# Projecting keys and values of a neighbourhood attention as one 512-column panel, with token rows as the stationary operand

## The chip, the cores and the metric

The kernel runs on one core of a Trainium2 chip. The metric is the device time of one execution in microseconds (us); the time before the change is the median of 3 runs. The compute engines are TensorE (PE in the rows; its weight loads PEld), VectorE (DVE), ScalarE (ACT) and GpSimd (POOL); SP only issues transfers.

## What is computed

Two transformer blocks in float32 over 256 tokens of width 2048. The first block (three mixers, an MLP of width 8192) and the second block's gated convolutional feed-forward are not touched. The change is in the second block's neighbourhood attention, over 256 tokens and 256 context rows, with 16 heads of 128:

```
def project(t):
    q, k, v = jnp.split(t @ w_qkv, 3, axis=-1)
    sh = (t.shape[0], t.shape[1], NA_HEADS, HEAD_DIM_2)
    return rms_norm(q.reshape(sh), q_g), rms_norm(k.reshape(sh), k_g), v.reshape(sh)

q, k, v = project(h)          # h: 256 own rows
qc, kc, vc = project(hc)      # hc: 256 context rows; only kc, vc are used
...
    logits = q @ [own keys, context keys] * scale + bias (own keys only)
    out = softmax(logits) @ [own values, context values]
y = out @ w_o
```

`c` and `c_ctx` go through `silu(cond) @ w_ada + b` (2048 x 12288) to give shifts, scales and gates; this product is worked on by VectorE beside the rest, piece by piece.

## The kernel before

**Weights as units.** All weights come as units of 128 x 1024 floats (512 KB) through a ring of four slots. For each unit SP loads `raw`, ScalarE copies it to `whi` (line 723, a rounded float32r), VectorE writes the rest `raw - whi` to `wlo` (line 1227), and TensorE uses it three times: whi with the high part of the activations, whi with their low part, wlo with the high part. `split(u0, m + 3)` on ScalarE may begin once TensorE is through with the unit three before (`unit_used`), on VectorE once `hi_done` says so; SP may refill `raw` after `lo_done`. The engines take their instructions in program order, and each program is written by hand: what stands behind a waiting instruction waits too.

**The attention phase** takes 8 turns of two heads each (`na_turn`), 12 units a turn: 4 of keys, 4 of queries, 4 of values, each 256 columns wide and 4 chunks of the contraction deep. Keys (units 0 to 3, lines 2486 and 2493) and queries (4 to 7, line 2498) have the weights stationary and the tokens moving, so that they come out turned, a head's 128 numbers on the partitions; keys move 512 tokens at a time, except in the last chunk and in the first turn (`first_keys`, line 2396), where own and context tokens stand apart and move 256. Values (8 to 11, line 2505) have 128 tokens stationary and 256 weight columns moving. Because a key's 128 numbers lie across partitions, the sums of squares for its norm come from a product with ones: ScalarE squares twice (1073, 1074), VectorE forms the low part (1779), TensorE multiplies (`norm_sums`, 2456 and 2457), ScalarE takes Ln and Exp (1057, 1059), VectorE scales (1744, 1748).

The attention of a turn's heads runs in the next turn: `attend_p(i, m)` behind unit m has the score product (2425), the transposes of the probabilities (2434) and the product with the values (2447); `attend_v` and `attend_a` are its halves on VectorE and ScalarE. The last turn's attention runs between the first units of `w_o` (`WO_UNITS`, line 1993, 32 units in four column groups n = 0 to 3, of 8 units each; a group adds into PSUM area q = n % 2).

**The w_ada product.** In each turn VectorE adds 32 terms (line 1559, 128x384) from 8 blocks of 4 terms. POOL loads a block (768 KB, line 655) into one of two buffers when the block two before is used up; behind the eighth load of a turn it adds a mask to the bias (661). `ada_tail` says which terms stand in which unit's slot. Behind the attention phase 16 more terms lie in `ffn_gate(j)`.

**The way into w_o.** The products with `w_o` need the heads' outputs in a high and a low part: ScalarE makes the high one (`heads_hi`, 1095), POOL the low one (689), in chunks; the units of group 0 wait for them (`a_lo`). VectorE adds a finished group to the residual (`add_gated`, 1827 and 1829), and the group two further on may not begin before 1827 has read the area (`drained`).

Of the kernel before, what the change touches and what calls it, by code (L numbers as in the profile page):

```python
# [19 lines left out]
F32 = mybir.dt.float32  # L20
F32R = mybir.dt.float32r
ACT = mybir.ActivationFunctionType
ALU = mybir.AluOpType
# [95 lines left out]
NA_OWN = 36  # L119
# [46 lines left out]
def program(nc, t, out):  # L166
    ctx = ExitStack()
    with ctx:
# [38 lines left out]
        ones_r = sb("ones_r", [P, P], F32R)  # L207


        with nc.sbuf_tensor("cst", [P, NCONST], F32) as cst, nc.sbuf_tensor("arena", [P, 17152], F32) as arena:  # L210
            pass
        first_dead = CONST["tri"][0]
        sb("kept_consts", [P, first_dead])
        nsq_hi = sb("nsq_hi", [P, 1024], F32R)
        sb("other_areas", [P, NCONST - first_dead - 1024 + 9472])
        nsq_lo = sb("nsq_lo", [P, 1024], F32R)
        sb("last_areas", [P, 17152 - 9472 - 1024])
# [56 lines left out]
        kT = area(4096, 2, 2 * S)  # L274
        vv = area(5120, 4, S)
# [4 lines left out]
        nsq = area(9472, 1024)  # L280
        nrs = area(10496, 1024)
# [46 lines left out]
        lr_ok = [sem(f"lr_ok{i}") for i in range(RING)]  # L328
# [39 lines left out]
        n_sq, n_nsum, n_rs, n_norm = (sem("na_" + n) for n in ("sq", "nsum", "rs", "norm"))  # L368
        n_sqa = sem("na_squares")
# [12 lines left out]
        D_NA = (D_MLP[0], D_MLP[1] + 8)  # L382
# [42 lines left out]
        def _(sp):  # L425
# [17 lines left out]
            for n, (name, c0, w) in enumerate(PANELS_IN):  # L443
                for j in range(8):
                    u = 8 * n + j
                    if name == "BV0":
# [4 lines left out]
                        sp.dma_start(dst[:, :, 0:LR], w_in[:, 2 * j:2 * j + 2, 3584:3600]).then_inc(lr_ok[j % RING], 16)  # L451
# [42 lines left out]
            with sp.Fori(1, 9) as i:  # L494
                for j in range(12):
                    first = (D, 0, 2 * D)[j // 4]
                    load(i * 12 + (U_NA - 12), j, raw[:, j % RING, :].rearrange("p (k n) -> p k n", n=256),
                         wq[:, 4 * (j % 4):4 * (j % 4) + 4, bass.ds(i * 256 + (first - 256), 256)])
            wo = t["na_w_o_2"][0].rearrange("(k p) n -> p k n", p=P)
            for i, (n, j) in enumerate(WO_UNITS):  # L500
                wide(U_WO, i, 512, wo[:, 2 * j:2 * j + 2, 512 * n:512 * n + 512])
# [197 lines left out]
        def _(act):  # L699
# [10 lines left out]
            act.sem_inc(n_rs, AHEAD)  # L710
# [165 lines left out]
            for m in range(8 * len(PANELS_IN)):  # L876
# [3 lines left out]
                if n < len(PANELS_IN):  # L880
                    name, _, w = PANELS_IN[n]
                    split(8 * n, j, w, (lr_ok[j % RING], 16 * (j // RING + 1)) if name == "BV0" else None)
                else:
                    split(8 * n, j)
# [94 lines left out]

            def turn_step(e, at):  # L980
# [14 lines left out]
            for j in range(4, 35):  # L995
                split(U_MLP + 3 * 64 + 32, j)
# [23 lines left out]
            split(U_NA, 3)  # L1020
# [10 lines left out]

            act.activation(ones_r[:, :], ones, ACT.Copy)
# [20 lines left out]
            def inv_rms(i, r):  # L1053
                v = nrs[:, 512 * (r % 2):512 * (r % 2) + 512]
                act.wait_ge(n_nsum, i * 3 + (r + 1))
                act.wait_ge(n_norm, i * 3 + ((1 if r == 2 else 0) + AHEAD))
                act.activation(v, X[2], ACT.Ln, scale=1.0 / NHD, bias=EPS).then_inc(n_rs, 1)
                act.wait_ge(n_rs, i * 6 + (2 * r + 1 + AHEAD))
                act.activation(v, v, ACT.Exp, scale=-0.5).then_inc(n_rs, 1)

            def na_turn(i, first):
                u0 = i * 12 + U_NA
                for m in range(12):
                    if not (first and m == 0):
                        split(u0, m + 3)
                    if m == 0 and not first:
                        act.wait_ge(unit_used, u0)
                        act.activation(vv, Gf[1].rearrange("p (c t) -> p c t", t=S), ACT.Copy).then_inc(drained[1], 1)
                    if not first:
                        attend_a(i, m)  # L1070
# [4 lines left out]
                    if m == 6:  # L1075
                        if first:
                            act.wait_ge(x2_ok, 1)
                        inv_rms(i, 0)
                    if m == 7:
                        inv_rms(i, 1)  # L1080
                    if m == 8:
                        act.wait_ge(unit_used, u0 + 8)
                        act.activation(nsq[:, 0:512], X[0], ACT.Square)
                        act.activation(nsq_hi[:, 0:512], X[0], ACT.Square).then_inc(n_sqa, 1)
                    if m == 10:
                        inv_rms(i, 2)

            na_turn(0, True)
            with act.Fori(1, 8) as i:
                na_turn(i, False)  # L1090
# [8 lines left out]
            act.wait_ge(unit_used, U_WO)  # L1099
            act.activation(vv, Gf[1].rearrange("p (c t) -> p c t", t=S), ACT.Copy).then_inc(drained[1], 1)  # L1100
            split(U_WO, 3)
            for m in range(7):
                attend_a(8, m, 1)
                if m < 6:
                    split(U_WO, 4 + m)
# [1523 lines left out]
```

## Time and profile before

| | |
|---|---|
| median of 3 runs | 2479.31 us (2478.68 to 2480.09) |
| the profiled execution's own time | 2479.1 us |
| its span | 2477.3 us |
| PE busy, granted clock | 2466.0 us (100%), 1.0 (2.4 GHz) in every stage read |
| DVE busy | 1781.5 us (72%) |
| ACT busy | 1183.1 us (48%) |
| POOL busy | 219.4 us (9%) |
| DMA | 519.08 MB, mean 210 GB/s |

The span lies 1.8 us inside the run's time. Busy time of PE is an envelope of overlapping matmuls, so a busy PE says little by itself; the order of its work and the waits in it have to be read.

### The profile page before, as it was taken

Reading aid. Unit: us, or ns where it says so; the run is one execution under the profiler, and the core shown is the slowest. Engines: PE = TensorE matmul, PEld = TensorE weight load, DVE = VectorE, ACT = ScalarE, POOL = GpSimd, SP = SyncE. Lnnn points to the kernel's source line nnn. Section 1 sums busy time; section 2 is a strip of 40 time slices with the busy share of each in tenths; the row PEclk is TensorE's granted clock in tenths of the full one; section 3 lists DMA queues with packets and bytes.
Section 4 is the critical chain, followed back from the end, with each engine's and each line's share of the span. In section 5 each row is a group of like instructions: output and inputs, shape, how many; then the busy total and the mean of one; then the engine's idle time right before and its main releaser. Section 6 shows DMA issues by size and latency. Waiting matters only on the chain.

```text
span 2477.3 us, 39343 instructions
## 1 busy us (share of the span) xinstructions
PE 2466.0 (100%) x14118; PEld 2156.9 (87%) x14118; DVE 1781.5 (72%) x2227; ACT 1183.1 (48%) x1517; POOL 219.4 (9%) x251
## 2 busy tenths in 40 slices
PE   9999999999999999999999999999999999999999
PEld 8989988888888888889999999988888888888887
DVE  6667657798887887786777777776766656665666
ACT  4455555544534535555333333354655435553453
POOL 5000000000000000223111111130200000000000
PEclk9999999999999999999999999999999999999999
DMA  8655577887787787764765565666556665566655
GB/s 270 186 132 150 172 247 231 296 278 254 240 285 243 249 282 238 259 213 151 219 189 188 186 194 183 199 211 191 189 179 197 193 191 181 182 198 193 187 182 173
DMA packets 279545, 519.08 MB, mean 210 GB/s; under 512 B 32750, under 2 KB 102648, under 8 KB 278672
## 3 DMA queue, kind: packets, MB, share of 16 engines
q1 hardware_dynamic: 254128, 403.66, 51.7%
q0 software_dynamic: 25120, 113.89, 14.8%
q8 instruction: 75, 1.23, 0.2%
q14 instruction: 30, 0.25, 0.0%
q10 hardware_dynamic: 192, 0.05, 0.0%
HBM read 515.35 MB, written 6.90 MB: 211 GB/s over the span
## 4 chain that ended last, share of the span: by engine, by line
PE 95%; DVE 2%; DMA 1%; issue 1%; ACT 0%; POOL 0%; DVEq 0%; ACTq 0%; POOLq 0%
PE ps L1993 33%; PE ps L2022 22%; PE ps L2025 11%; PE ps L2505 7%; PE ps L2493 6%; PE ps L2498 4%; PE ps L1985 3%; PE ps L2447 1%; PE ps L2425 1%; PE ps L2396 1%; DVE wlo L1227 1%; PE ps L2314 1%; PE ps L2434 1%; PE ps L2486 0%; DMA raw<-in_w_in 0%
## 5 line engine op out<-in xcount | busy, mean ns | idle before, releaser
L1227 DVE TENSOR_TENSOR wlo<-raw,whi 128x1024 fp32r<-128x1024 f32 (+1 forms) x776 | 939.6, 1222 | 419.0 <-ACT whi L723 402.3
L723 ACT ACTIVATE whi<-raw 128x1024 fp32r<-128x1024 f32 (+1 forms) x776 | 798.5, 1037 | 797.3 <-PE ps L1993 355.2
L1993 PE MATMUL ps<-whi,act 128*128 128x512 f32 (+3 forms) x2736 | 821.9, 382 | 0.9 <-DVE wlo L1227 0.9
L2022 PE MATMUL ps<-act,whi 128*128 128x512 f32 x2400 | 657.6, 395 | 1.4 <-DVE act L1867 1.3
L1993 PEld LDWEIGHTS ps<-whi,act 128*128 128x128 f32 x2736 | 504.4, 188 | 92.2 <-issue 3.2
L1993 PE MATMUL ps<-wlo,act 128*128 128x512 f32 (+3 forms) x1368 | 519.3, 380 | 0.0
L2022 PEld LDWEIGHTS ps<-act,whi 128*128 128x128 f32 x2400 | 410.1, 189 | 56.6 <-DVE act L1867 1.6
L2025 PEld LDWEIGHTS ps<-act,wlo 128*128 128x128 f32 x2400 | 369.5, 189 | 51.7
L2025 PE MATMUL ps<-act,wlo 128*128 128x256 f32 x2400 | 383.9, 281 | 0.0
L1993 PEld LDWEIGHTS ps<-wlo,act 128*128 128x128 f32 x1368 | 256.9, 188 | 45.1
L1559 DVE SCALAR_TENSOR_TENSOR arena<-arena,cond 128x768 f32<-128x768 f32 (+1 forms) x330 | 284.2, 884 | 12.2 <-DMA arena<-in_w_ada 8.9
L2505 PE MATMUL ps<-whi,act 128*128 128x256 f32 x1024 | 185.8, 284 | 0.0
L2505 PEld LDWEIGHTS ps<-whi,act 128*128 128x128 f32 x1024 | 160.3, 191 | 1.4
L2505 PE MATMUL ps<-wlo,act 128*128 128x256 f32 x512 | 144.9, 283 | 0.0
L2493 PE MATMUL ps<-act,whi 128*128 128x512 f32 x420 | 131.7, 395 | 0.0
L601 POOL DMA_DIRECT2D arena<-in_w_ada x64 | 46.4, 724 | 663.8 <-DVEq L1577 586.8
L2505 PEld LDWEIGHTS ps<-wlo,act 128*128 128x128 f32 x512 | 97.8, 191 | 0.0
L1038 ACT ACTIVATE arena<-arena,nst 128x512 f32<-128x512 f32 x32 | 23.2, 726 | 155.3 <-DVE nst L1732 155.3
L1985 PE MATMUL ps<-act,whi 128*128 128x256 f32 x512 | 95.5, 287 | 0.6 <-DVE act L1246 0.6
L2498 PE MATMUL ps<-act,whi 128*128 128x256 f32 x512 | 95.0, 286 | 0.0
L1906 DVE SCALAR_TENSOR_TENSOR arena<-arena,cols 128x255 f32<-128x255 f32 x172 | 71.9, 480 | 31.6 <-ACT arena L1162 28.0
L2493 PEld LDWEIGHTS ps<-act,whi 128*128 128x128 f32 x420 | 76.9, 188 | 14.8
(332 smaller groups left out, 2142.1 us busy)
## 6 DMA issues: line engine op xcount, KB each, us to landing
arena<-in_w_ada POOLq DMA_DIRECT2D x128, 768.0 KB, 6.1
raw<-in_ffn_w_up SPq DMA_DIRECT2D x160, 512.0 KB, 4.2
raw<-in_w_mlp_in SPq DMA_DIRECT2D x128, 512.0 KB, 4.9
raw<-in_w_mlp_out SPq DMA_DIRECT2D x128, 512.0 KB, 5.5
raw<-in_na_w_qkv SPq DMA_DIRECT2D x96, 512.0 KB, 4.7
raw<-in_ffn_w_down SPq DMA_DIRECT2D x84, 512.0 KB, 4.4
raw<-in_w_in SPq DMA_DIRECT2D x64, 384.0 KB, 3.8
raw<-in_w_in SPq DMA_DIRECT2D x32, 512.0 KB, 4.4
```

Source lines behind the costliest of these rows:

```text
L601: pool.dma_start(ada1[:, e % 4, :, :], wa[:, 2 * e:2 * e + 2, bass.ds(s * ADA_W, ADA_W)])\
L723: act.activation(a, b, ACT.Copy).then_inc(hi_done, 1)
L1227: dve.tensor_tensor(a, b, c, ALU.subtract).then_inc(lo_done, 1)
L1559: return dve.scalar_tensor_tensor(out=acc, in0=piece, scalar=sc, in1=acc, op0=ALU.mult, op1=ALU.add)
L1906: ins = dve.scalar_tensor_tensor(out=a, in0=b, scalar=w, in1=a, op0=ALU.mult, op1=ALU.add)
L1985: ins = pe.matmul(o, a, b, start=start and i == 0, stop=last and i == 2, skip_group_check=True)
L1993: ins = pe.matmul(o, a, b, start=start and i == 0, stop=last and i == 2, skip_group_check=True)
L2022: pe.matmul(Z[q][:, c, :].rearrange("p (h t) -> p h t", h=2), kn(whi, j)[:, kk, P * c:P * c + P], act2[:, :, k, 0:S], start=k == 0, stop=k ...
L2025: ins = pe.matmul(Z[q][:, c, 0:S], kn(wlo, j)[:, kk, P * c:P * c + P], ahi[:, k, 0:S], start=False, stop=k == KC - 1, skip_group_check=True)
L2493: ins = pe.matmul(G[0][:, c, :], a, b, start=st and y == 0, stop=False, skip_group_check=True)
L2498: ins = pe.matmul(X[0][:, S * c:S * c + S], a, b, start=st and y == 0 and c == 0, stop=sp_ and y == 2, skip_group_check=True)
L2505: ins = pe.matmul(Gf[1][:, S * r:S * r + S], a, b, start=st and y == 0 and r % 2 == 0, stop=sp_ and y == 2, skip_group_check=True)
```

## The change

Keys and values become one panel: a unit holds 2 chunks of the contraction and 512 columns (256 of keys, 256 of values), and with 128 tokens stationary the 512 columns move past. Units 0 to 7 are such panels, over four token tiles, in PSUM banks 0 to 3; units 8 to 11 are the queries, also with tokens stationary. Each panel unit is loaded by two transfers, with a semaphore (`part_ok`) beside `raw_full`; so are the first three units of `w_o`. Keys and queries now lie with a token's numbers along a row: VectorE sums the squares there (`row_sums`), ScalarE makes the factor, VectorE scales, and TensorE turns the result head by head (`turn_keys` behind unit 10, `turn_queries` behind unit 0 of the next turn), 8 and 4 transposes; the gains are applied by the copies out of PSUM (`k_out`, `q_out`). The product with ones is gone. The attention of a turn begins one unit later; the last turn's begins behind unit 2 of `w_o`, not ahead of unit 0. The w_ada terms are placed anew (`FIRST_TERMS`, `TURN_TERMS`, `ffn_gate`), and groups 0 and 1 of `w_o` end only at units 14 and 15.

```
-WO_UNITS = [(n, j) for n in range(4) for j in range(8)]
-WO_UNITS[7], WO_UNITS[8] = WO_UNITS[8], WO_UNITS[7]
-FIRST_TERMS = {7: range(16, 19), 8: range(19, 23), 9: range(23, 27), 10: range(27, 30), 11: range(30, 32)}
+WO_UNITS = [(n, j) for n in (0, 1) for j in range(7)] + [(0, 7), (1, 7)] + [(n, j) for n in (2, 3) for j in range(8)]
+FIRST_TERMS = {3: range(16, 19), 4: range(19, 22), 5: range(22, 25), 6: range(25, 28), 7: range(28, 32)}
+TURN_TERMS = [range(0, 3), range(3, 6), range(6, 9), range(9, 12), range(12, 15), range(15, 19), range(19, 23), range(23, 28),
+              range(28, 29), range(29, 30), range(30, 31), range(31, 32)]
...
# ScalarE, the turn
-                    if m == 4:
-                        act.wait_ge(unit_used, u0 + 4)
-                        act.activation(nsq, Gf[0], ACT.Square)
-                        act.activation(nsq_hi[:, :], Gf[0], ACT.Square).then_inc(n_sqa, 1)
...
                     if m == 8:
                         act.wait_ge(unit_used, u0 + 8)
+                        if not first:
+                            act.wait_ge(n_o, i * 4 + AHEAD)
+                        for r in range(4):
+                            act.activation(kv[:, r, :], ps[:, r, :], ACT.Copy).then_inc(k_row, 1)
+                    if m == 9:
+                        inv_rms(16, k_rms, i * 2 + 1, 8)
+                    if m == 11:
+                        act.wait_ge(k_turn, i + 1)
+                        act.activation(kT, ps[:, 5:7, :], ACT.Copy, scale=cols[:, R_KG:R_KG + 1]).then_inc(k_out, 1)
...
# VectorE, the turn
+            def row_sums(rows_, sums, r):
+                for a in range(2):
+                    at = 2 * r + a
+                    v = rows_[:, NHD * a:NHD * a + NHD]
+                    if at >= 4:
+                        own.wait(3)
+                    own.mark(dve.tensor_tensor_reduce(n_junk[:, at % 4, :], v, v, 1.0, 0.0, ALU.mult, ALU.add,
+                                                      nst[:, sums + at:sums + at + 1]))
...
+                    if m == 8:
+                        key_sums(i)
+                    if m == 9:
+                        key_norm(i)
...
-                        attend_v(i, m)
-                        ada_tail(i, m)
+                        if m == 0:
+                            query_norm(i)
+                        else:
+                            attend_v(i, m - 1)
+                        ada_terms(i, TURN_TERMS[m])
...
# VectorE beside w_o
-                if 11 <= j < 19:
-                    ada_terms(8, range(2 * j - 22, 2 * j - 20))
+                if 13 <= j < 19:
+                    ada_terms(8, ((0, 1, 2), (3, 4, 5), (6, 7, 8), (9, 10, 11), (12, 13), (14, 15))[j - 13])
...
-                if j % 8 == 3:
-                    n = j // 8 - 1
+                if j in (18, 19, 27):
+                    n = (18, 19, 27).index(j)
                     dve.wait_ge(gate_in, 16)
-                    add_gated(n, n % 2, U_WO + (9 if n == 0 else 8 * n + 8), drained[n % 2], D_NA[n % 2] + n // 2 + 1, gb)
+                    add_gated(n, n % 2, U_WO + (15, 16, 24)[n], drained[n % 2], D_NA[n % 2] + n // 2 + 1, gb)
...
# TensorE
+            def key_value_unit(m, tiles):
+                for kk in range(2):
+                    k = 2 * m + kk
+                    wh, wl = kn(whi, m)[:, kk, :], kn(wlo, m)[:, kk, :]
+                    for r in tiles:
+                        for y, (a, b) in enumerate(terms(wh, wl, tile_rows(r, 0, k), tile_rows(r, 1, k), False)):
+                            ins = pe.matmul(ps[:, r, :], a, b, start=k == 0 and y == 0, stop=k == KC - 1 and y == 2,
+                                            skip_group_check=True)
+                return ins
...
             def first_keys():
-                pe.wait_ge(drained[0], D_MLP[0])
+                for q in range(2):
+                    pe.wait_ge(drained[q], D_MLP[q])
...
-                if i < 6:
-                    attend_p(8, i + 1, 1)
+                if i == 1:
+                    turn_queries(8)
+                if 2 <= i <= 8:
+                    attend_p(8, i - 2, 1)
```

VectorE in the first turn, from slot 7 (a split, L1227 before and L1240 now; the w_ada terms are L1559 before and L1572 now). Before:

```order
L1227 TENSOR_TENSOR wlo<-raw,whi 128x1024 [waits hi_done]
L1744 SCALAR_TENSOR_TENSOR arena<-ps,cols,arena 128x512 [waits na_rs]
L1227 TENSOR_TENSOR wlo<-raw,whi 128x1024 [waits hi_done]
L1558 TENSOR_SCALAR arena<-arena,cond 128x384 [waits ada_in0]
L1559 SCALAR_TENSOR_TENSOR arena<-arena,cond 128x384 [waits dve_step] x2
L1744 SCALAR_TENSOR_TENSOR arena<-ps,cols,arena 128x512 [waits na_rs,dve_step]
```

Now, with the sums of squares as L1759 (the row of the sum and the row of its accumulator) and the scaling as L1766:

```order
L1240 TENSOR_TENSOR wlo<-raw,whi 128x1024 [waits hi_done,ada_done]
L1572 SCALAR_TENSOR_TENSOR arena<-arena,cond 128x384 [waits ada_in1]
L1572 SCALAR_TENSOR_TENSOR arena<-arena,cond 128x384 [waits dve_step] x3
L1240 TENSOR_TENSOR wlo<-raw,whi 128x1024 [waits hi_done,ada_done]
L1759 ISA arena,nst<-arena 128x128 [waits na_keys_rows]
L1759 ISA nst 128x1
```

```order
L1240 TENSOR_TENSOR wlo<-raw,whi 128x1024 [waits dve_step,hi_done]
L1766 TENSOR_TENSOR arena<-arena,nst 128x4x256 [waits na_keys_sums_rms]
L1240 TENSOR_TENSOR wlo<-raw,whi 128x1024 [waits hi_done] x2
L159 UNCONDITIONAL_BRANCH
L159 ISA
```

The keys' norm used to stand ahead of most terms; now all 16 terms of this turn, with the wait for the last block (`ada_in1`), stand ahead of the eight sums and of the scaling.

TensorE in the turn, behind the third of the last four units (queries now, values before). Before:

```order
L2505 MATMUL ps<-wlo,act2 128x256
L2456 MATMUL ps<-nsq_hi,ones_r 128x512 [waits na_rs,na_pt,na_sq]
L2457 MATMUL ps<-nsq_lo,ones_r 128x512
L2505 MATMUL ps<-whi,act2 128x256 [waits lo_done]
L2505 MATMUL ps<-whi,act2 128x256
```

Now:

```order
L2483 MATMUL ps<-cst,arena 128x128 [waits na_pt,na_logits,na_keys_scaled]
L2483 MATMUL ps<-cst,arena 128x128 x7
L2527 REGISTER_ALU
L2446 MATMUL ps<-whi,act2 128x256 [waits lo_done]
L2446 MATMUL ps<-whi,act2 128x256
```

At this place TensorE now waits for the scaled keys of the same turn.

VectorE beside w_o, around the first add of a finished group (L1827 before, L1863 now). Before:

```order
L1807 TENSOR_TENSOR act2<-arena,act2 128x2x256 [waits a_hi,a_lo]
L1227 TENSOR_TENSOR wlo<-raw,whi 128x1024 [waits hi_done] x2
L1827 TENSOR_TENSOR arena<-ps,arena 128x1024 [waits unit_used,gate_rows_in]
L1829 TENSOR_TENSOR x<-x,arena 128x2x512 [waits drained0]
L1558 TENSOR_SCALAR acc3<-arena,cond 128x384 [waits dve_step,ada_in0]
```

Now:

```order
L1240 TENSOR_TENSOR wlo<-raw,whi 128x1024 [waits hi_done,dve_step]
L1572 SCALAR_TENSOR_TENSOR acc3<-arena,cond,acc3 128x384
L1572 SCALAR_TENSOR_TENSOR acc3<-arena,cond,acc3 128x384 [waits dve_step] x2
L1240 TENSOR_TENSOR wlo<-raw,whi 128x1024 [waits hi_done,ada_done]
L1572 SCALAR_TENSOR_TENSOR acc3<-arena,cond,acc3 128x384 [waits ada_in1]
L1572 SCALAR_TENSOR_TENSOR acc3<-arena,cond,acc3 128x384 [waits dve_step]
L1240 TENSOR_TENSOR wlo<-raw,whi 128x1024 [waits hi_done,dve_step]
L1863 TENSOR_TENSOR arena<-ps,arena 128x1024 [waits unit_used,gate_rows_in]
L1865 TENSOR_TENSOR x<-x,arena 128x2x512 [waits drained0]
```

The add of group 0 stood ahead of all 16 terms; it now stands behind 14 of them.

## Rows read from the trace of the kernel before

**Rows 1.** The page: shares of the chain that ended last

```profile
PE 95%; DVE 2%; DMA 1%; issue 1%; ACT 0%; POOL 0%; DVEq 0%; ACTq 0%; POOLq 0%
```

**Rows 2.** Waits in the attention phase and w_o, longest first (total, times, longest)

```profile
PE ps L2425 <- DVE arena L1729: 1.4, 3, 0.5
...
PE ps L1993 <- DVE wlo L1227: 0.3, 1, 0.3
```

**Rows 3.** The chain in order of time, in a turn (start, us, work)

```profile
1343.82 2.87 PE ps L2498 x24
...
1384.73 5.49 PE ps L2493 x24
1390.22 0.86 PE ps L2425 x2
1391.08 0.44 PE ps L2434 x4
```

**Rows 4.** The chain where the MLP hands over to the first turn

```profile
1113.50 1.42 DVE x L1544 x2
...
1118.03 0.21 ACT frms L1016
...
1119.24 1.06 PE ps L2386 x8
```

**Rows 5.** VectorE in order of time, one turn (start, us, operation, idle before)

```profile
1228.24 2.58 DVE L1559 SCALAR_TENSOR_TENSOR arena<-arena,cond 128x384 f32<-128x384 f32 x4
1232.26 2.92 DVE L1227 TENSOR_TENSOR wlo<-raw,whi 128x1024 fp32r<-128x1024 f32 x1 [1.44 <-ACT whi L723]
```

**Rows 6.** POOL in the same turn

```profile
1231.46 0.75 POOL L655 DMA_DIRECT2D arena<-in_w_ada  x1 [4.64 <-DVE arena L1559]
1232.23 1.85 POOL L661 TENSOR_TENSOR arena<-arena,cst 128x768 f32<-128x768 f32 x1
```

**Rows 7.** Row sums of squares, 128x192 (min/median/max ns, first and last start)

```profile
L1434 DVE CUSTOM_DVE_ANT_0 arena<-x x8: 352/354/355, 287.9 to 289.8; 128x192 f32<-128x192 f32 x8
```

**Rows 8.** Loads of w_ada blocks: from turn 2 on; then those beside w_o

```profile
DMA to landing us min/median/max: 4.9/5.2/7.6
DMA to landing us min/median/max: 7.6/7.6/7.6
```

**Rows 9.** First turn: loads of blocks 5, 6 and 7, and POOL's last issues

```profile
DMA to landing us min/median/max: 9.5/9.5/9.5
DMA to landing us min/median/max: 8.5/8.5/8.5
DMA to landing us min/median/max: 10.9/10.9/10.9
1166.61 0.75 POOL L655 DMA_DIRECT2D arena<-in_w_ada  x1 [4.97 <-issue]
1169.16 1.19 POOL L671 DMA_DIRECT2D gate_row_scratch<-mods  x1
```

**Rows 10.** w_o with the last attention: VectorE, ScalarE, POOL

```profile
1650.68 0.42 DVE L1727 SCALAR_TENSOR_TENSOR arena<-ps,arena 128x256 f32<-128x256 f32 x1
1654.04 0.71 ACT L1095 ACTIVATE act<-arena 128x256 fp32r<-128x256 f32 x2
1654.53 2.14 POOL L689 TENSOR_TENSOR act<-arena,act 128x256 fp32r<-128x256 f32 x2 [3.38 <-ACT act L1095]
```

**Rows 11.** VectorE in the later part of w_o

```profile
1689.69 1.22 DVE L1227 TENSOR_TENSOR wlo<-raw,whi 128x1024 fp32r<-128x1024 f32 x1
1690.84 1.26 DVE L1559 SCALAR_TENSOR_TENSOR acc<-arena,cond,acc 128x384 f32<-128x384 f32 x2
...
1697.63 1.27 DVE L1559 SCALAR_TENSOR_TENSOR acc<-arena,cond,acc 128x384 f32<-128x384 f32 x2 [1.83 <-DMA arena<-in_w_ada]
...
1707.41 1.22 DVE L1827 TENSOR_TENSOR arena<-ps,arena 128x1024 f32<-128x1024 f32 x1
```

**Rows 12.** The chain in w_o: three units in a row, behind the attention

```profile
1675.18 8.22 PE ps L1993 x36
```

More of the change, by code:

```diff
@@ L366, in program @@
             ("bias", "scores", "logits", "max", "exp", "probs", "turned", "pt", "pv", "out"))
[L368 to L369 removed]
+        k_row, k_rms, k_norm, k_turn, k_out = (sem("na_keys_" + n) for n in ("rows", "sums_rms", "scaled", "turned", "out"))
+        q_row, q_rms, q_norm, q_turn, q_out = (sem("na_query_" + n) for n in ("rows", "sums_rms", "scaled", "turned", "out"))
         gate_cols, gate_out, gate_in = sem("gate_columns"), sem("gate_row_out"), sem("gate_rows_in")
@@ L1019, in _ @@
             scale_piece(1, xs, xs, frms[:, 1, 0:1])
-            split(U_NA, 3)
+            split(U_NA, 3, extra=key_part(0, 3))
             turn_step(4, 0)
@@ L1671, in _ @@
                     own.done(ins)
-            own.done(dve.tensor_tensor_reduce(ps[:, 3, :], xs[:, 1, cs3], xs[:, 1, cs3], 1.0, 0.0, ALU.mult, ALU.add, fsq[:, 3, 3:4]))
+            own.done(dve.tensor_tensor_reduce(area(7424, 512), xs[:, 1, cs3], xs[:, 1, cs3], 1.0, 0.0, ALU.mult, ALU.add, fsq[:, 3, 3:4]))
             dve.wait_ge(fsq_ok, 1)
@@ new lines, in rows_scaled, with query_norm @@
+            def rows_scaled(v, sums, n, done):
+                by = nst[:, sums + n:sums + 2 * n].rearrange("p (r h) -> p r h", h=2).unsqueeze(3).to_broadcast([P, n // 2, 2, NHD])
+                v = v.rearrange("p r (h n) -> p r h n", n=NHD)
+                dve.tensor_tensor(v, v, by, ALU.mult).then_inc(done, 1)
+            def query_norm(i):
+                dve.wait_ge(q_row, i)
+                for r in range(RT):
+                    row_sums(qr[:, r, :], 32, r)
+                own.wait()
+                dve.sem_inc(q_rms, 1)
+                dve.wait_ge(q_rms, i * 2)
+                rows_scaled(qr, 32, 4, q_norm)
@@ L1755, in ada_terms, with key_sums, key_norm @@
+            def key_sums(i):
+                for r in range(4):
+                    dve.wait_ge(k_row, i * 4 + (r + 1))
+                    row_sums(kv[:, r, 0:S], 16, r)
+                own.wait()
+                dve.sem_inc(k_rms, 1)
+            def key_norm(i):
+                dve.wait_ge(k_rms, i * 2 + 2)
+                rows_scaled(kv[:, :, 0:S], 16, 8, k_norm)
             def ada_terms(i, ks):
@@ L2507, in na_turn @@
-                    ins.then_inc(unit_used, 1)
-                    if not first:
-                        attend_p(i, m)
-                    if m == 0:
+                    pe.wait_ge(lo_done, u0 + (m + 1))
+                    if first and m < 8:
+                        pe.wait_ge(a_lo, TURN_AT[4] + 2 * m + 2)
+                    if m < 8:
+                        key_value_unit(m, range(4)).then_inc(unit_used, 1)
+                    else:
+                        if m == 8 and not first:
+                            pe.wait_ge(q_row, i)
+                        query_unit(m)
@@ L2516, in na_turn @@
                     if m == 10:
-                        norm_sums(i, 2)
+                        turn_keys(i, first)
             na_turn(0, True)
```

273 lines of the change are left out of this document (112 added, 161 removed).

## The prediction, written before the changed kernel was run

> **What bounds the kernel now.** First the page's shares of the chain that ended last: TensorE holds 95% of it [rows 1]. Then the waits of the attention phase: from the first turn to the end of w_o TensorE waits four times, 1.4 us for VectorE's logits and 0.3 for weights, all in w_o [rows 2]. Then the chain in order of time, which gives the pitch at which TensorE takes each kind of work at full clock: 24 matmuls of 512 columns in 5.49 us are 0.228 us each, 24 of 256 columns in 2.87 us are 0.120 us, a product with ones, as wide, the same, a score product 0.86 us, four transposes 0.44 us, 0.11 each [rows 3]. In w_o 36 matmuls of 512 columns take 8.22 us, again 0.228 [rows 12]. So in the turns TensorE's own list of work is the time, and each microsecond taken from it counts, as long as nothing new makes it wait. VectorE is busy 49 of a turn's 67 us, but in bursts, and its order decides below.
>
> **The work on TensorE.** A steady turn before has 90 projection matmuls of 512 columns and 300 of 256: 20.5 + 36.0 = 56.5 us. Now 192 of 512 and 96 of 256: 43.8 + 11.5 = 55.3 us. The columns streamed are the same; what is saved is 0.012 us for each of 102 pairs of 256 that became one of 512, 1.2 us. Six products with ones (1.4 us) go, twelve transposes (1.3 us) come. Net -1.25 us a turn, -8.8 us over seven. In the first turn all 480 matmuls were 256 wide (57.6 us), so 2.3 us are saved, 1.4 go and 8 transposes (0.9) come: -2.8 us. The last queries' four transposes fall into w_o: +0.4 us. Sum -11.2 us, and this would be the result if every wait were covered. The Trainium skill speaks against the saving: its page "TensorE: Matmul & The Clock Gate", section "Back-to-back issue gap", puts an isolated gap at the columns over 2.4 plus about 2.5 ns, by which a pair would save 2.5 ns and a turn 0.3 us. The rows show 12 ns a pair, so the rows stand [rows 3].
>
> **The hand-over into the first turn, +1.5 us.** Before, TensorE went from the last MLP matmul straight into the first context half, since only area 0 had to be free. Now it waits for `drained[1]` as well, which VectorE sets behind its last add, 1.42 us from 1113.50 [rows 4]. The other wait there, for the scaled rows, ended at 1119.24 just as two context halves had run; it no longer adds anything, as TensorE arrives later.
>
> **Turning the keys in a steady turn, +2.2 us each.** Unit 7 starts at 0, when the last product with the values is done. TensorE: unit 7 to 5.5, unit 8 and one w_ada turn to 8.7, units 9 and 10 to 14.4; then `turn_keys` wants the scaled keys. VectorE was waiting in slot 6 for that same product, since the copy of the output stands ahead of slot 6's terms. From 0: copy 0.45, terms 19 to 22 at 0.645 each [rows 5], 19 done at 1.1 and all at 3.05, split 1.14 (back to back), term 23 at 4.85. Term 24 needs block 6, whose load POOL can issue once term 19 is done. POOL takes 0.64 us to react (terms that end at 1230.82, issue at 1231.46 [rows 5, 6]), and a block lands 5.2 us later [rows 8]: 6.9. Meanwhile POOL issues block 7 (term 23 frees it, 5.5 to 6.25) and adds the mask, 1.85 us, to 8.1. That mask add has a price: the split that met it took 2.92 instead of 1.22 us, till 1.1 us behind POOL's end [rows 5, 6]. The four terms will now meet it, so they begin at 8.1 and end at 10.7. Then split 11, to 11.85; eight row sums, for which 128x192 gives a pitch of (289.8-287.9)/7 = 0.27 us [rows 7], less 64 elements, 0.21: 13.55; ScalarE's Ln and Exp, 0.45 [rows 4], beside term 28 to 14.2; split 12 to 15.4; the scaling of 128x1024, priced as a split of that size, to 16.6. TensorE waits 2.2 us, more than the 1.25 saved: +0.95 a turn, +6.7 over seven.
> Bounds: if the mask does not hold the terms up, the wait is 1.0 us and the turn gains 0.3; if block 6 were there in time as well, no wait and -1.25; with the 7.6 us landing [rows 8] the wait is 3.5. I take the block, as both operations read two SBUF operands like the split. The skill's page "SBUF — State Buffer", section "SBUF: two separate sides", says so: a VectorE operation with two SBUF inputs and a GpSimd one that reads SBUF lock each other out for a whole instruction. The split's row agrees with it; that a term is held the same way no single row shows.
> The two transfers in place of one for each panel unit cost nothing that I can see: they move the same bytes in the same 1 KB pieces, and are issued in the slot four ahead of ScalarE's use, behind which a 5 us landing hides; the extra wait on ScalarE falls on a semaphore long set. The queries' path holds: 5.5 us of unit 0 against split 1.1 + 1.2, sums 0.85, Ln/Exp 0.45, scaling 0.7, about 4.6 us.
>
> **Turning the keys in the first turn, +6.3 us.** All 16 terms stand ahead of the sums here. `x2_ok` frees POOL at about 1143, as before; block 5, issued at about 1144.8, lands 9.5 us later as it did [rows 9], so term 20 goes at 1154.3; three more terms and a split at the prices above put term 23's end at 1158.1 and block 7's issue at 1158.7. Before, this block needed 10.9 us, with the gate's row being written 2.55 us behind its issue [rows 9]; the same order stands on POOL now. Landed at 1169.6, terms 28 to 31 end at 1172.2, split 1173.3, sums 1175.0, split 1176.1, scaling 1177.3. TensorE, 1.5 us late at the start and then without a wait, wants them at 1171.0. Bounds: 0.5 us if the block lands in 5 us, 3.9 with block 6's 8.5 [rows 9].
>
> **w_o with the last attention, +2.3 us.** Unit j of group 0 needs chunks 2j and 2j+1 of the heads. Before, from VectorE's start on a score product to POOL's two low parts passed 5.99 us (1650.68 to 1656.67 [rows 10]), and TensorE had two units and two score products to fill it. Now the attention comes two units later but the chunks' places on ScalarE do not, so only one unit, a score product and transposes (about 3.9 us) stand between: unit 4 waits 2.4 us, units 2, 5 and 6 together 1 us. Unit 0 waits 1.0 us too, since `heads_hi` now stands behind the copy of the keys. Against these 4.4 us, the waits there before were 2.2 us (1.4 listed [rows 2], the rest in modelled ends). +2.2, rounded with the queries' turn 2.7 in all.
>
> **w_o, group 2, +5.6 us.** Call T the start of unit 9. TensorE reaches unit 16, the first of group 2, at T+19.2 (seven units of 2.74 [rows 12]) and needs the first half of `add_gated(0)`. VectorE: split 13 cannot end before T+5.1 (its high part needs unit 9's end); three terms 6.85; split 8.0; term 3 at 8.65, which frees block 2's buffer; issue 0.3 later as at 1689.97, landing 7.6 us [rows 8]: 16.6. Terms 4 to 7 and a split are done by 12.4; it waits. Term 8 at 17.25, split 18.4, three terms 20.35, split 21.5, two terms 22.8, split 23.95, then the multiply of 1.22 [rows 11]: 25.2. TensorE waits 6.0. Before, that add stood at unit 11, five units ahead of need, and its own wait for the block, 1.83 us idle [rows 11], was absorbed. With a landing of 5.2 the wait is 3.6. About 0.4 is given back where TensorE waited 0.3 us for weights [rows 2]: that wait is behind unit 16.
>
> **Sum.** -2.8 + 1.5 + 6.3 = +5.0 for the first turn, +6.7 for seven, +2.7 and +5.6 for w_o: +20.0 us on the profiled execution's 2479.1, 1.8 of which lie outside its span. It stands 0.2 below the median: 2499.
>
> **The rivals.** A change under 0.2% (5 us) cannot be told from none here.
> (1) Slower as above, the waits outweighing the work: 70%. Its own range 2485 to 2508.
> (2) Covered waits, faster: only the work and the hand-over count, -11.2 + 1.5, 2469. It would need the terms not to hold the norm, by block landings of under 4.2 us or a mask that costs nothing, and group 0's add in time. Against it: no landing of under 4.9 us in [rows 8], and group 2 waits 1.7 us even without any block wait. With some of the waits it ends between: 2469 to 2474. 15%.
> (3) The lower ends together: first turn -2.8 + 1.5 + 0.5, seven turns -2, w_o +2.7 + 3.2: +3, 2482. Within 0.2%. 15%.
> (4) The change doesn't save what it says, because 512 columns over the stationary rows take twice 0.120: +9.8 us on top, 2509. The same form runs at 0.228 in w_o [rows 12]; this is inside the slower chance, under 3%.
>
> **How the numbers follow.** Likeliest case 2499. The range reaches down to take in most of (3), 2478, and up to the longer landings (7 x 1.3 + 8 in w_o), 2508. Faster 0.15, same 0.15, slower 0.70.
>
> **What will show it.** In the changed profile: projection pieces of 5.48 us and 2.87 us, work per turn 66.1; TensorE idle behind unit 10 with the scaling (VectorE, the new line 1766) as releaser, about 2 us in seven turns and 4 to 6 in the first; a wait of 3 to 6 us at unit 16 of w_o for VectorE's 1863; a wait for the low parts before unit 4; a period of 68.3 us a turn against 67.3. I am wrong if the turn's period is 66.1 (the terms never hold the norm), or if the group wait is missing, which would mean blocks that land far sooner.

## The result, and the profile after

The changed kernel takes 2518.61 us (median of 4 runs, 2516.8 to 2520.29), the kernel before 2479.12 in the same comparison: a ratio of 1.0156, 95% interval 1.0144 to 1.0168. It is slower by 39.5 us where 20 were predicted, and lies outside the range given. In one of the runs below, run 10, one of 8 executions took 8167 us and is left out of the ratio.

TensorE's share of the chain that ended last, 95% before [rows 1], is now:

```profile
PE 88%; DVE 5%; DMA 4%; issue 2%; ACT 1%; POOL 0%; DVEq 0%; SPq 0%; POOLq 0%; ACTq 0%
```

TensorE's waits from the hand-over to the end of w_o (total, times, longest), where before there were 1.4 and 0.3 us [rows 2]:

```profile
PE ps L2483 <- DVE arena L1766: 21.1, 8, 3.4
PE ps L2029 <- POOL act L694: 5.7, 5, 2.5
PE ps L2472 <- DVE arena L1766: 5.0, 1, 5.0
PE ps L2029 <- DVE arena L1863: 5.0, 1, 5.0
PE ps L2435 <- issue: 1.6, 1, 1.6
```

Four of these five were predicted, with 21.7, 4.4, 6.0 and 1.5 us. The third was not: the turning of the first queries, behind unit 0 of turn 1. The stages, from the starts of the units in the chain, in microseconds of the profiled executions (the last one ends where TensorE begins the feed-forward's products, at 1749.3 before and at 1788.5 after):

| stage | before | after | more | predicted |
|---|---|---|---|---|
| to the start of turn 1 | 1176.1 | 1181.4 | +5.3 | +5.0 |
| turn 1 | 67.3 | 78.2 | +10.9 | +0.95 |
| turns 2 to 6 | 336.6 | 345.8 | +9.2 | +4.75 |
| turn 7 and w_o | 169.3 | 183.1 | +13.8 | +9.25 |

One steady turn in the chain in order of time, to set beside [rows 3]:

```profile
1378.44 4.89 DMA arena<-in_w_ada
1383.36 1.74 DVE arena L1572
...
1391.20 0.93 issue
1392.13 1.23 DVE arena L1766
1393.40 1.09 PE ps L2483 x8
1394.50 2.88 PE ps L2446 x24
1397.38 5.47 PE ps L2435 x24
```

This is the predicted path, link by link: block 6 lands, term 24 (1.74 us instead of 0.63) goes under the mask add, three terms, split, sums and scaling follow, and TensorE waits 2.52 us for it (2.2 predicted). Counted from the start of unit 7 at 1376.45, block 6 lands at 6.9, its four terms end at 10.6 and the scaling at 16.9, where the prediction has 6.9, 10.7 and 16.6. Around the first turn's end, ScalarE, and then POOL, in order of time:

```profile
1178.09 1.06 ACT L727 ACTIVATE whi<-raw 128x1024 fp32r<-128x1024 f32 x1 [5.11 <-DMA raw<-in_na_w_qkv]
1185.38 1.06 ACT L727 ACTIVATE whi<-raw 128x1024 fp32r<-128x1024 f32 x1 [6.23 <-DMA raw<-in_na_w_qkv]
...
1188.29 0.58 ACT L1069 ACTIVATE arena<-ps 128x512 f32<-128x512 f32 x1
```

```profile
1162.74 1.19 POOL L676 DMA_DIRECT2D gate_row_scratch<-mods  x1
```

ScalarE stands 11.3 us before weights that have not landed, and the copy of the queries' rows (1069) stands behind the second of these splits. The landing of the write at 1162.74 (8 KB, the gate's row), and of the second transfers of the units requested at 1164.6 and 1167.7:

```profile
DMA to landing us min/median/max: 12.5/12.5/12.5
```

```profile
DMA to landing us min/median/max: 13.4/15.5/17.6
```

Then TensorE's clock. The windows of the changed kernel (us, then busy time of PE, PEld, DVE, ACT, POOL; the last three numbers are granted clock, DMA share, GB/s), and two pieces of the chain:

```profile
1165.00:1170.00 5.00, 5.00 (x44) 5.00 (x43) 4.79 (x8) 1.98 (x4) 0.77 (x1) 1.00 0.42 29
1170.00:1175.00 5.00, 1.56 (x15) 1.36 (x13) 4.80 (x19) 0.42 (x2) 0.75 (x1) 0.86 0.50 32
1175.00:1180.00 5.00, 5.00 (x24) 5.00 (x25) 0.82 (x1) 1.06 (x1) 0.00 (x0) 0.50 0.96 283
...
1190.00:1195.00 5.00, 3.12 (x11) 2.84 (x12) 3.94 (x12) 2.15 (x4) 0.00 (x0) 0.57 0.47 157
```

```profile
1532.28 4.31 PE ps L2446 x24
```

```profile
1739.77 10.27 PE ps L2029 x36
```

Two things are to be seen. While the 8 KB write is under way the DMA engines are half busy (0.42 and 0.50) and move 29 to 32 GB/s. And behind TensorE's stall the granted clock is 0.50, its lower level (1.2 GHz), for a few microseconds: 24 matmuls of 256 columns take 4.31 us instead of 2.87 [rows 3], 36 of 512 take 10.27 instead of 8.22 [rows 12]. Such pieces stand behind the first turn's wait, the queries' wait in turn 1, the keys' wait of turns 1 and 5, and the wait of group 2.

### The profile page after: what moved, and what is told of

It is laid out like the page before. It is cut to its first block, busy times and chain, and to the rows that moved or that the text cites. A ratio compares the mean times of both kernels' runs of the same rounds, so it can differ in the third digit from the quotient of the medians.

```text
span 2516.6 us, 38054 instructions
## 1 busy us (share of the span) xinstructions
PE 2468.2 (98%) x13260; PEld 2119.8 (84%) x13260; DVE 1786.5 (71%) x2395; ACT 1161.1 (46%) x1512; POOL 218.1 (9%) x251
## 4 chain that ended last, share of the span: by engine, by line
PE 88%; DVE 5%; DMA 4%; issue 2%; ACT 1%; POOL 0%; DVEq 0%; SPq 0%; POOLq 0%; ACTq 0%
PE ps L2029 33%; PE ps L2058 22%; PE ps L2061 11%; PE ps L2435 11%; PE ps L2021 3%; DMA arena<-in_w_ada 2%; DVE arena L1572 2%; PE ps L2513 1%; PE ps L2494 1%; DVE wlo L1240 1%; PE ps L2446 1%; DMA raw<-in_na_w_qkv 1%; DMA raw<-in_w_in 1%; PE ps L2503 1%; PE ps L2350 0%
## 5 line engine op out<-in xcount | busy, mean ns | idle before, releaser
L1240 DVE TENSOR_TENSOR wlo<-raw,whi 128x1024 fp32r<-128x1024 f32 (+1 forms) x776 | 930.4, 1210 | 411.8 <-ACT whi L727 390.2
L2029 PE MATMUL ps<-whi,act 128*128 128x512 f32 (+3 forms) x2736 | 823.8, 382 | 11.3 <-POOL act L694 5.7
L2058 PE MATMUL ps<-act,whi 128*128 128x512 f32 x2400 | 657.6, 395 | 1.4 <-DVE act L1903 1.3
L2029 PEld LDWEIGHTS ps<-whi,act 128*128 128x128 f32 x2736 | 505.0, 188 | 104.5 <-POOL act L694 5.7
L2058 PEld LDWEIGHTS ps<-act,whi 128*128 128x128 f32 x2400 | 410.1, 189 | 56.6 <-DVE act L1903 1.6
L2435 PE MATMUL ps<-whi,act 128*128 128x512 f32 x1024 | 325.0, 399 | 1.6 <-issue 1.6
L1572 DVE SCALAR_TENSOR_TENSOR arena<-arena,cond 128x768 f32<-128x768 f32 (+1 forms) x330 | 291.2, 905 | 19.4 <-DMA arena<-in_w_ada 16.0
L2435 PEld LDWEIGHTS ps<-whi,act 128*128 128x128 f32 x1024 | 189.5, 189 | 42.1 <-issue 5.3
L2435 PE MATMUL ps<-wlo,act 128*128 128x512 f32 x512 | 201.1, 393 | 0.0
L606 POOL DMA_DIRECT2D arena<-in_w_ada x64 | 46.3, 724 | 665.0 <-DVEq L1590 588.2
L2446 PE MATMUL ps<-whi,act 128*128 128x256 f32 x512 | 98.8, 294 | 0.0
L2021 PE MATMUL ps<-act,whi 128*128 128x256 f32 x512 | 95.5, 287 | 0.6 <-DVE act L1259 0.6
L2446 PEld LDWEIGHTS ps<-whi,act 128*128 128x128 f32 x512 | 83.8, 199 | 0.6
L660 POOL DMA_DIRECT2D arena<-in_w_ada x64 | 48.2, 753 | 413.3 <-DVE acc L1572 226.3
```

Of the source, the lines that this page charges most:

```text
L606: pool.dma_start(ada1[:, e % 4, :, :], wa[:, 2 * e:2 * e + 2, bass.ds(s * ADA_W, ADA_W)])\
L660: pool.dma_start(ada2[:, q % 2, :, :], wa[:, 4 * c:4 * c + 4, bass.ds(i * 768 + (6144 + (s - 1) * TAIL_W), TAIL_W)])\
L1240: dve.tensor_tensor(a, b, c, ALU.subtract).then_inc(lo_done, 1)
L1572: return dve.scalar_tensor_tensor(out=acc, in0=piece, scalar=sc, in1=acc, op0=ALU.mult, op1=ALU.add)
L2021: ins = pe.matmul(o, a, b, start=start and i == 0, stop=last and i == 2, skip_group_check=True)
L2029: ins = pe.matmul(o, a, b, start=start and i == 0, stop=last and i == 2, skip_group_check=True)
```

## The experiments

Each is timed against the kernel before in the same comparison; its ratio is to that kernel. Where a time is said to be so many us less, it is less than the changed kernel's 2518.61 us. Letters A, B and C are the rivals of the expectation quoted.

**1. The gate row's write, later.**

```
             attention_loads(0, range(4, 8))
+            attention_loads(1)
             gate_row_out(0, 32)
-            with pool.Fori(1, 8) as i:
+            with pool.Fori(2, 8) as i:
```

> The changed kernel (2518.6 us) with one edit: the write of the gate's row (8 KB out of 128 partitions) is issued behind the loads of turn 1 instead of behind those of the first turn. Theory A: this write, which took about 12 us to land and began 6.4 us earlier than before the change, holds up the unit loads behind it; ScalarE's two waits for weights (11.3 us) and the 5.0 us of TensorE at the turning of the first queries come from it. Then turn 1 falls from 78.4 to 68.9 to 70 us, and the time by 8 to 10, to 2509 to 2511. Rival B: the loads are late because the w_ada blocks of the first turn are loaded earlier and the panel units come as two transfers; then turn 1 stays above 76 us and the time within 2 us of 2518.6. Rival C: the write does the same harm wherever it stands; then the loss moves to turn 2 and the time stays.

Measured: 2514.5 us, ratio 1.0148 (1.0131 to 1.0165), 4 us less. Turn 1 takes 74.0 us. The first transfers of the three units requested from 1164.5 to 1171.4 now land in:

```profile
DMA to landing us min/median/max: 3.0/5.0/5.9
```

and the queries' wait of 5.0 us is gone. But in turn 1 the keys' wait is 5.1 instead of 2.5. POOL, then VectorE, there:

```profile
1234.17 0.75 POOL L660 DMA_DIRECT2D arena<-in_w_ada  x1 [3.09 <-DVE arena L1573]
...
1236.73 1.19 POOL L676 DMA_DIRECT2D gate_row_scratch<-mods  x1
```

```profile
1245.30 0.62 DVE L1573 SCALAR_TENSOR_TENSOR arena<-arena,cond 128x384 f32<-128x384 f32 x1 [3.06 <-DMA arena<-in_w_ada]
```

Block 7, on its way when the write begins, takes 11 us, and the norm stands behind its first term. So A holds for what the write does at the first turn's end. The time lies between A's (8 to 10 us less) and C's (none), and the 4 us are hardly clear of noise: the four executions span 2512.87 to 2521.42 us. The write still harms what is in transit beside it and soon needed.

**2. Four terms behind the norm** (`TURN_TERMS` from slot 7: term 23; none; 24 to 27; 28 and 29; 30 and 31).

> The changed kernel with terms 24 to 27 of turns 1 to 7 moved behind the scaling of the keys (slot 9), 28 and 29 to slot 10, 30 and 31 to slot 11. Theory A: the 2.5 us wait of TensorE at the turning of the keys is the norm standing behind block 6 and its four terms; it vanishes in turns 1 to 7, a steady turn takes 66.2 us instead of 68.9, and with two places at which the granted clock had fallen behind that wait (1.5 us each) the time falls by 19 to 22 us, to 2497 to 2500. Rival B: the split for unit 11, now beside POOL's mask, takes the place of the terms and the scaling is late all the same: periods of 68, the time 2512 to 2516. Rival C: the late terms delay the next turn's first block, and the next turn's terms or splits hold TensorE up: periods of 67 to 69 with waits at another place.

Measured: 2514.79 us, ratio 1.0144 (1.0127 to 1.0161), against an expected 2497 to 2500: a miss. TensorE's waits in steady turns:

```profile
PE ps L2472 <- DVE arena L1766: 10.2, 5, 2.1
```

There is no wait for the keys any more, as A said, but one of 2.05 us for the queries, and a turn takes 68.4 us. Between the two scalings (of the keys, then of the queries) VectorE now has eight terms besides its splits, where it had three, and the queries' sums stand behind them. This is rival C, with a time in B's range. The norm has two deadlines in 10 us, and terms pushed past the first meet the second.

**3. The mask add behind block 5** (`if q == 5:` in place of 7).

> The changed kernel with POOL's mask add issued behind block 5 of a turn instead of block 7. Theory A (the step of the prediction): VectorE's terms 24 to 27 took 3.9 us instead of 2.6 because this add holds them; without it they take 2.6, TensorE's wait at the turning of the keys falls from 2.5 to about 1.2 us, a turn from 68.9 to 67.6, and the time by 9 to 12 us, to 2507 to 2510. Rival B: the terms are slow for another reason (they read a block that has just landed while others land): they stay at 3.9 us and the time within 2 us of 2518.6.

Measured: 2504.75 us, ratio 1.0102 (1.0085 to 1.0119), 13.9 less. VectorE's terms 24 to 27, in the changed kernel and in this one:

```profile
1383.36 3.69 DVE L1572 SCALAR_TENSOR_TENSOR arena<-arena,cond 128x384 f32<-128x384 f32 x4 [1.99 <-DMA arena<-in_w_ada]
```

```profile
1375.10 2.58 DVE L1572 SCALAR_TENSOR_TENSOR arena<-arena,cond 128x384 f32<-128x384 f32 x4 [2.03 <-DMA arena<-in_w_ada]
```

A holds for the mechanism: the terms are back at 2.58 us with the block still 2 us late, and the wait is 1.3 to 1.7 us; the prediction had put this bound at 1.0. No slow piece stands behind these shorter waits in turns 1 to 7. The first turn pays: with the mask add gone from between them, the row's write stands right behind block 7's request, the block lands in 10.2 us instead of 4.9, and the keys' wait there is 7.0 us, so that turn 1 starts 3.3 us later. TensorE then comes later to the turning of the first queries, and the wait there (5.0 us, with 2.8 of slow pieces behind it) is gone. This trade gives 4.5 of the 14.5 us between the two profiled executions; some 10 are the mask add's.

**4. Both adds ahead of 12 of the 16 terms beside w_o** (terms 0 to 3 in slots 13 and 14, the rest two a slot from 19 on; their sums at slot 26; their turn on TensorE at unit 22).

> The changed kernel with only 4 of the 16 w_ada terms of w_o ahead of the two adds of groups 0 and 1 (slots 13 and 14); the other 12 stand behind them, two per slot, and their sums follow at slot 26. Theory A: TensorE's 5.0 us wait at the first unit of group 2 is the add behind 14 terms and a block's load, and the 1.8 us that the units behind it take longer is the granted clock that fell in that wait; both vanish, 6.8 us, to 2512. Rival B: the coefficients and the gate's row of the feed-forward come later now and its first products wait for them: the 5.0 us at group 2 are gone but the time falls by under 3 us.

Measured: 2513.27 us, ratio 1.0138 (1.0121 to 1.0155), 5.3 less. TensorE's waits in w_o:

```profile
PE ps L2029 <- POOL act L694: 4.3, 4, 2.5
PE ps L2029 <- DVE wlo L1240: 1.8, 1, 1.8
PE ps L2350 <- DVE acc L1572: 1.1, 1, 1.1
PE ps L2029 <- DVE arena L1863: 0.9, 1, 0.9
```

The wait for the add falls from 5.0 to 0.9 and the slow piece is gone, as A said; two new waits give 2.9 back: TensorE is at the terms' turn before they are done, and the second gate row's write, at 1757.0, is now nearer the end of w_o; ScalarE waits 6.4 us for weights behind it, as it did before this edit, but TensorE has less left to cover that. The time, between A's and B's, is no proof by itself: of the 5.4 us between the two profiled executions, 2.7 lie ahead of turn 2, where this edit changes nothing (the queries' wait is 3.3 us there instead of 5.0).

**5. The heads' high parts early** (chunks 4 to 8 and 9 to 13 in the first two slots of w_o).

> The changed kernel with ScalarE's high parts of the heads (chunks 4 to 13) made in the first two slots of w_o instead of two per slot over five. Theory A: TensorE's waits for POOL's low parts (5.7 us in five places: 1.5 at unit 0, then 0.8, 2.5, 0.3, 0.6) come, but for the first, from the places of the high parts; those behind the first vanish, 4.2 us, and the time falls by 4 to 5 us, to 2514. Rival B: POOL itself is the limit there (1.08 us a chunk, 14 chunks) and is in use until about 1690 whatever ScalarE does, or the score products' chain becomes the wait: the time falls by less than 2 us.

Measured: 2514.53 us, ratio 1.0139 (1.0122 to 1.0156), 4.1 less. Of the waits for low parts there is left:

```profile
PE ps L2029 <- POOL act L694: 0.8, 1, 0.8
```

A holds in the main: the waits of 2.5, 0.6 and 0.3 us are gone, and POOL's own pace was not their limit. The one of 0.8 stays, against A, and the 1.5 at unit 0 is only hidden here, since turn 7's last unit ran at the lower clock (4.32 us) and TensorE came later; run 7 shows both again.

**6. Term 19 one slot earlier** (slots 5 to 7: 15 to 19, 20 to 23, 24 to 27).

> The changed kernel with one w_ada term moved in turns 1 to 7: term 19, which frees block 4's buffer, stands in slot 5 instead of slot 6, ahead of the wait for the product with the values; slots 6 and 7 then have terms 20 to 23 and 24 to 27. Theory A: block 6 is requested some 5 us earlier and has landed when term 24 is due, and the norm is on time: no wait at the turning of the keys, a steady turn of 66.2 to 66.5 us instead of 68.9, the time 18 to 21 us less, 2498 to 2501. Rival B: the mask add still holds the terms and the split, and 1.0 to 1.5 us of the wait stay: 2507 to 2511. Rival C, as the run with terms behind the norm did: the wait goes to the turning of the queries and the turn stays above 68.

Measured: 2502.52 us, ratio 1.009 (1.0074 to 1.0107), 16.1 less; the keys' wait is 0.64 us in each of seven turns and a turn takes 66.98 us. The block is there in time, but the mask add still holds the terms. VectorE in the same slot of run 7, whose turns are the same:

```profile
1361.56 4.41 DVE L1576 SCALAR_TENSOR_TENSOR arena<-arena,cond 128x384 f32<-128x384 f32 x4
```

1.84 us more than the 2.57 without it, and the mask add takes 1.86. So most of A and a part of B, and a time between theirs.

**7 and 8. All of it together; and the early write alone, in the kernel before.** Run 7 has the edits of runs 4 (the terms' turn on TensorE at unit 23), 5 and 6, the terms of the first turn thinned (28 to 31 behind the keys' scaling), and both rows' writes moved to where few loads are due; the second waits for unit 29 of w_o, the first for the end of the first turn:

```
+            attention_loads(1, range(2))
+            pool.wait_ge(unit_used, U_NA + 12)
             gate_row_out(0, 32)
+            attention_loads(1, range(2, 8))
-            with pool.Fori(1, 8) as i:
+            with pool.Fori(2, 8) as i:
```

> The changed kernel with all of it together: term 19 a slot earlier; in the first turn terms 28 to 31 behind the key norm (slots 10 and 11), 22 to 27 thinned; the gate row's write issued once TensorE is through the first turn, ahead of turn 1's third block; high parts early in w_o; both adds ahead of 12 of the 16 terms beside w_o, and the second row's write issued when unit 29 of w_o is done. Theory A: the cost of the change is only waits and transfers, and its work on TensorE is 11.2 us less than before. Left are 1.6 at the hand-over, about 1.5 at unit 0 of w_o and 1 to 3 in the first turn: 2471 to 2476, faster than the kernel before (2480). Rival B: what was saved at one place comes back at another, as it did in two of the four runs so far: 2480 to 2495.

Measured: 2477.91 us, ratio 0.9989 (0.9979 to 0.9998), a time between A's and B's. Run 8 is the kernel before with its own write earlier:

> The kernel before the change with one edit: the write of the gate's row is issued ahead of the first turn's last block instead of behind it (about 1160 instead of 1169 us), where it stands in time in the changed kernel. If the write's place alone decides, unit loads are late by as much here too, TensorE waits 5 to 10 us around the start of turn 1 and the kernel takes 2484 to 2490. If the write only harms together with the change's own transfers and clock, the time stays within 2 us of 2480.

Measured: 2481.34 us, ratio 1.0004 (0.9995 to 1.0014). Run 7's waits:

```profile
PE ps L2487 <- DVE arena L1770: 4.5, 7, 0.8
PE ps L2033 <- POOL act L697: 2.3, 2, 1.5
PE ps L2439 <- issue: 1.6, 1, 1.6
PE ps L2033 <- DVE arena L1867: 0.9, 1, 0.9
```

All of the 39.5 us are gone. In run 8 the write goes out at the same time as in the changed kernel, and here too a unit load lands late, the second of these two:

```profile
DMA to landing us min/median/max: 3.6/9.4/15.2
```

```profile
PE ps L2318 <- DVE arena L1563: 1.0, 1, 1.0
```

yet TensorE waits only 1.0 us there, and the time is that of the kernel before within the interval. The write's place alone is not the cause.

**9 and 10. What was left, and the write put back.** Run 9 is run 7 with the mask add behind block 5 in turns 1 to 7, run 10 is run 7 with the first write where the change has it.

> The kernel with all waits covered (2477.9 us) and, in turns 1 to 7, POOL's mask add behind block 5. There the mask add holds terms 24 to 27 of each turn in full (4.4 us for four instead of 2.57, 1.84 more, the mask add itself 1.86), and TensorE waits 0.65 us for the scaling in each turn. Theory A: the terms take 2.57, the wait is gone in seven turns, a steady turn is 66.3 us instead of 66.98, and the time 4 to 5 us less: 2473 to 2474, 0.3% under the kernel before. Rival B: the mask add now meets other terms or splits in slots 4 and 5, which then make TensorE wait: the time stays within 1 us of 2477.9.

> The kernel with all waits covered (2477.9 us), but the write of the first gate row where the change has it, behind the first turn's last block. Theory A: with the queries' short units (2.9 us each) at the end of the turn, three units are requested while this write is under way, and they land late whatever VectorE's order is: TensorE waits 3 to 7 us around the start of turn 1, 2481 to 2486. Rival B: the loads were only late because VectorE's splits, behind its terms, freed the buffers late; with the terms thinned out the write is harmless: within 1.5 us of 2477.9.

Run 9: 2471.34 us, ratio 0.9968 (0.9956 to 0.998), 8 us under the kernel before and 2 below A's range. VectorE's four terms and the chain of a turn, from one turning of the keys to the next, and the waits left up to the end of w_o:

```profile
1425.52 2.57 DVE L1576 SCALAR_TENSOR_TENSOR arena<-arena,cond 128x384 f32<-128x384 f32 x4
```

```profile
1369.51 0.87 PE ps L2487 x8
1370.38 2.88 PE ps L2450 x24
1373.26 5.47 PE ps L2439 x24
...
1435.64 0.87 PE ps L2487 x8
```

```profile
PE ps L2033 <- POOL act L697: 1.8, 2, 1.5
PE ps L2439 <- issue: 1.6, 1, 1.6
PE ps L2033 <- DVE arena L1867: 0.9, 1, 0.9
```

A turn takes 66.13 us without a wait. Run 10: 2486.02 us, ratio 1.0026 (1.0016 to 1.0037): against run 7 the write's place costs 8.1 us (9 by the two ratios) in a kernel in which little else is late. A holds, at the upper end of its times and with a longer wait (7.9 us) than its 3 to 7. ScalarE, and TensorE's longest wait:

```profile
1184.09 1.06 ACT L728 ACTIVATE whi<-raw 128x1024 fp32r<-128x1024 f32 x1 [10.36 <-DMA raw<-in_na_w_qkv]
```

```profile
PE ps L2473 <- DVE arena L1767: 7.9, 1, 7.9
```

## Why the prediction was half right

**The work on TensorE, -8.8 us in seven turns: right.** Without waits a turn takes 66.13 us (run 9) against 67.32: -1.19 each, -8.3. The 12 ns for a merged pair came from the rows. A turn also trades six products for twelve transposes, which the rows put at -0.1. By the isolated gap that the Trainium skill's page "TensorE: Matmul & The Clock Gate" states in its section "Back-to-back issue gap", a pair saves 2.5 ns; an estimate from it, with the same trade, is 67.0 us a turn. The measurement decides for the rows.

**The hand-over, +1.5: right**, 1.6.

**The keys in a steady turn, +0.95 each: mechanism right, +1.55 measured.** The wait is 2.52 us, not 2.2. Each of its two causes was taken away alone: the block's lateness (run 6) and the mask add (run 3). That the mask add holds a term as it held the split had no row of its own before; now it has: four terms take 1.84 us longer beside a mask add of 1.86 (run 7 against run 9). The Trainium skill's page "SBUF — State Buffer", section "SBUF: two separate sides", states an exclusive lock between a VectorE operation with two SBUF inputs and a GpSimd one that reads SBUF, and the traces agree. The 0.6 us a turn by which the sum was short are 0.3 in the wait, 0.1 in the work and 0.2 in the eight transposes behind the wait, which take 1.09 us there and 0.87 without a wait (run 9). The 9.2 us of turns 2 to 6 are five times 1.55 and 1.4 at a slow unit.

**The keys in the first turn, +6.3: the wrong block, 3.4 measured, and the sum right by luck.** The prediction has VectorE wait for block 7. Block 7 landed 4.9 us after its request, the lower bound, not the 10.9 of [rows 9], and VectorE never waited for it. With its request at 1160.2 and the write 2.5 us behind it, nearly all of it seems to have been in before the write began to hurt. That the margin is thin run 3 shows, with the write 0.7 us behind the request and a landing of 10.2. But a landing of 5 us should have left a wait of 0.5 by the prediction's own bound. The rest of the 3.4 comes from two things that the sum for this turn lacks: VectorE stood 1.6 us before block 6, and POOL's mask add, at 1160.95, held a split for 3.12 us instead of 1.22:

```profile
1160.13 0.62 DVE L1572 SCALAR_TENSOR_TENSOR arena<-arena,cond 128x384 f32<-128x384 f32 x1 [1.60 <-DMA arena<-in_w_ada]
1160.78 3.12 DVE L1240 TENSOR_TENSOR wlo<-raw,whi 128x1024 fp32r<-128x1024 f32 x1
...
1166.91 2.57 DVE L1572 SCALAR_TENSOR_TENSOR arena<-arena,cond 128x384 f32<-128x384 f32 x4
```

The last line is block 7's four terms, with no idle time before them. The 2.9 us by which 3.4 is under 6.3 are lost again to the clock: unit 11 takes 4.8 us instead of 3.1 in TensorE's own rows, and the transposes 0.9 more than in a steady turn.

**The queries' path, "holds: 4.6 of 5.5 us": the step that failed.** It was priced for a steady turn, where it does hold, and never asked for turn 1, nor was ScalarE's queue in it: the copy of the queries' rows stands behind two splits, and these behind weights. +10.9 us instead of +0.95: 5.0 of wait, 1.9 and 1.5 us of slow units behind this wait and the keys', 0.9 in slow transposes, and the 1.55 of every turn. The cause is the gate's row's write, as runs 1 and 10 show, where it meets something that the change brought. What that is was argued, not tried alone; the likeliest is the units' length. The queries' units, 2.9 us each, stood in the middle of the turn and now stand at its end, so in 8.6 us from 1162.8 three units are used up and their successors requested, and there the gate's row is being written, 12.5 us long. Before, the values' units stood there (48 matmuls at the 0.120 us of [rows 3], 5.8 us each), and a load of 15 us cost TensorE a wait of 1 us (run 8). Run 10 shows the write's price at 8.1 us with VectorE's lateness taken out. The prediction had this write in its rows and used it only for block 7's landing. The rival is that each unit there is now loaded by two transfers where it was one; in run 1, away from the write, these land in 3 to 6 us, but no run has one transfer a unit beside the write. Whether they cost nothing, as predicted, stays open.

**The clock, not in the sum at all.** The slow pieces are 1.9, 1.5, 1.4 and 2.0 us in the chain, 1.7 at unit 11 and 1.4 in transposes: some 10 us, a quarter of the loss. Every price was taken at full clock, since before the granted clock was 1.0 in every stage; a forecast of new waits should have priced what follows a wait.

**w_o, +8.3: +12.2 measured.** The waits for low parts are 5.7 us instead of 4.4, of which the high parts' place cures 3.4 (run 5); group 2 waits 5.0 instead of 6.0, and pays 2.0 in clock. The range's lower case, with the shortest waits together, was nowhere near; the upper end, 2508, lacked both the write and the clock.

## What to carry to other kernels

When a change reorders units of unequal length, look at what the transfer queues carry where the short ones now stand: here four units of 2.9 us seem not to hide what two of 5.8 did. Price a new wait with its echo: 2.5 us of TensorE's idling cost up to 4 with the slow matmuls behind it, and shortening it below that got both back. A filler term may stand in front of one deadline or of the next; moving the request of its data (one term, one slot earlier: 16 us) did more than moving the terms (4 us).

## What was not expected of the hardware

The write of 8 KB, 16 columns out of 128 partitions turned into a row, took 11.5 to 13.2 us to land at five places, before and after and in runs 9 and 10 (10.0 in run 1), and while it runs other transfers move at 29 to 32 GB/s instead of the 283 of the window behind it: unit loads of 256 KB need 12.6 to 17.6 us instead of 3 to 6 (run 1). And of seven waits of 2.52 us in the changed kernel's turns, two were followed by matmuls at the lower clock level and five were not; behind the waits of 0.65, 1.3 to 1.7 and 2.05 us in turns 1 to 7 of runs 6, 3 and 2 there was none, behind those of 3.3 us and more there always was one. Which of the 2.52 us waits it follows is not fixed: the turns' code is the same in runs 1, 4 and 5, where it follows in turns 4 and 7, in 1, 4 and 7, and in 1, 3 and 7.
